# Twenty-four instead of twenty rounds of value sums beside the gates of a PEER layer

## The reference, cut to what matters

```python
experts = jnp.take_along_axis(cand_idx..., top_pos, axis=-1)   # 8 heads x 16 = 128 experts per token
gates = jax.nn.softmax(top_s, axis=-1)
def apply_block(args):                                         # one tile of 128 tokens
    xs, es, gs = args
    u = expert_u[es]; vv = expert_v[es]                        # tables of 16384 rows of 1024
    a = jax.nn.gelu(jnp.einsum('tkd,td->tk', u, xs), approximate=False)
    return jnp.einsum('tk,tkd->td', gs * a, vv)
```

## Time and profile before

| | us |
|---|---|
| median of 3 runs | 1929.65 (1924.39 to 1934.65) |
| the profiled execution | 1945.27 |
| its span | 1943.5 |
| around the span | 1.8 |
| PE busy | 1795.4 (92%) |
| DVE busy | 1292.2 (66%) |
| POOL busy | 896.7 (46%) |
| ACT busy | 293.5 (15%) |
| DMA moved | 670.21 MB, mean 345 GB/s |

### The profile page before, as it was taken

The page is one execution under the profiler, slowest core; times in us unless marked ns, Lnnn a source line. Parts: engine busy times, 40 slices in busy tenths (PEclk is TensorE's granted clock), DMA queues, the critical chain, the costliest instruction groups (busy, mean ns, idle before and its releaser), DMA issues.

```text
span 1943.5 us, 21544 instructions
## 1 busy us (share of the span) xinstructions
PE 1795.4 (92%) x8020; PEld 1152.3 (59%) x8020; DVE 1292.2 (66%) x2593; ACT 293.5 (15%) x661; POOL 896.7 (46%) x837
## 2 busy tenths in 40 slices
PE   4988898998999999998999999996889999999994
PEld 1666743554444359987888888884554444444441
DVE  2110476989579699998998975568875623336767
ACT  0120010555100001111111100005550000000000
POOL 1010225665456324334455555668865665435540
PEclk9999999999999999998999999998999999999998
DMA  8895859888999977559999999999989999999995
GB/s 360 338 370 214 344 160 394 291 286 324 392 324 363 390 272 298 187 192 362 366 361 375 386 387 409 405 394 329 327 308 409 409 409 409 409 409 409 409 410 203
DMA packets 168441, 670.21 MB, mean 345 GB/s; under 512 B 19563, under 2 KB 19691, under 8 KB 163085
## 3 DMA queue, kind: packets, MB, share of 16 engines
q0 software_dynamic: 112512, 410.79, 56.2%
q1 hardware_dynamic: 51072, 242.25, 31.8%
q10 hardware_dynamic: 4752, 15.81, 2.1%
HBM read 659.27 MB, written 7.39 MB: 343 GB/s over the span
## 4 chain that ended last, share of the span: by engine, by line
PE 46%; DMA 18%; DVE 18%; POOL 11%; issue 6%; ACT 1%; ACTq 0%; DVEq 0%; another core or an unknown queue 0%; POOLq 0%
PE psum L966 19%; POOL arena L566 11%; DMA arena<-in_expert_u_dram,arena 9%; DMA arena<-in_expert_v_dram,arena 4%; DVE arena L1511 4%; PE psum L751 4%; PE psum L992 3%; PE psum L995 3%; DVE psum L1784 3%; PE psum L740 2%; PE psum L1029 2%; DVE arena L1707 2%; DMA arena<-in_w_ada_dram 2%; PE psum L1006 2%; PE psum L1004 2%
## 5 line engine op out<-in xcount | busy, mean ns | idle before, releaser
L566 POOL DMA_INDIRECT arena<-in_expert_u_dram,arena x384 | 468.5, 1220 | 386.0 <-DVE arena L1511 261.6
L1511 DVE CUSTOM_DVE_ANT_0 arena<-arena 128x1024 f32<-128x1024 f32 x384 | 461.0, 1222 | 182.1 <-DMA arena<-in_expert_u_dram,arena 153.0
L566 POOL DMA_INDIRECT arena<-in_expert_v_dram,arena x384 | 390.7, 1018 | 357.9 <-DVE psum L1784 175.9
L1784 DVE SCALAR_TENSOR_TENSOR psum<-arena,psum 128x1024 f32<-128x1024 f32 x254 | 327.0, 1287 | 193.2 <-DMA arena<-in_expert_v_dram,arena 165.0
L893 PE MATMUL psum<-arena 128*128 128x256 f32 x2048 | 446.0, 381 | 7.3 <-DMA arena<-in_expert_uT_dram 7.3
L966 PE MATMUL psum<-arena 128*128 128x512 f32 x1024 | 443.7, 594 | 1.6 <-DMA arena<-in_expert_v_dram 1.6
L893 PEld LDWEIGHTS psum<-arena 128*128 128x128 f32 x2048 | 390.8, 191 | 61.3 <-issue 7.6
L966 PEld LDWEIGHTS psum<-arena 128*128 128x128 f32 x1024 | 193.3, 190 | 253.0 <-issue 249.0
L1064 PE MATMUL psum<-arena 128*128 128x128 f32 x1280 | 148.9, 278 | 2.1 <-DVE arena L1668 1.4
L1064 PEld LDWEIGHTS psum<-arena 128*128 128x128 f32 x1280 | 147.1, 194 | 3.6 <-issue 1.9
L1324 ACT ACTIVATE arena<-psum 128x512 f32<-128x512 f32 x64 | 38.2, 597 | 379.7 <-PE psum L893 292.6
(11 more groups left out here) (188 smaller groups left out, 1410.1 us busy)
## 6 DMA issues: line engine op xcount, KB each, us to landing
arena<-in_expert_uT_dram SPq DMA_DIRECT2D x128, 512.0 KB
arena<-in_expert_v_dram SPq DMA_DIRECT2D x128, 512.0 KB
arena<-in_w_ada_dram SPq DMA_DIRECT2D x12, 2048.0 KB
arena<-in_w_in_dram SPq DMA_DIRECT2D x11, 2048.0 KB
arena<-in_w_query_dram SPq DMA_DIRECT2D x8, 2048.0 KB, 22.7
arena<-in_w_in_dram SPq DMA_DIRECT2D x30, 512.0 KB, 7.9
arena<-in_w_o_dram SPq DMA_DIRECT2D x4, 2048.0 KB
arena<-in_expert_u_dram,arena POOLq DMA_INDIRECT x384
```

The source lines that it names most:

```text
L566: pool.indirect_dma_start(slot, None, table[0], bass.IndirectOffsetOnAxis(ap=number, axis=0)).then_inc(land, 16)
L1511: dve.tensor_tensor_reduce(UR[b], UR[b], U2B[e], 1.0, 0.0, ALU.mult, ALU.add, DOTS[e % 2][:, k:k + 1]).then_inc(u_free, 1)
L1784: dve.scalar_tensor_tensor(ys, row, weight, ys, ALU.mult, ALU.add).then_inc(v_free, 1)
```

## The change

`GATE_ROUNDS` becomes 24. So rounds 0 to 23 go beside the gates, three after each four batches, and rounds 24 to 31 go into the value stream. `ROUND_AFTER` before names the blocks 33, 35, 38, 42, 46, 50, 55, 59, 63, 67, 72 and 76; after it names 38, 40, 43, 47, 51, 55, 60 and 64. From the constants follow `BESIDE` (48 before, 32 after), `PACED_FROM` (76, then 64) and `PACE` (43, then 55), so the paced fetches are 96 in 55 blocks instead of 80 in 43. Both paces end at the same block, 119.

```diff
-SCORED_GROUPS, GATE_ROUNDS = 10, 20
+SCORED_GROUPS, GATE_ROUNDS = 10, 24
 BESIDE = ROUND * (ROUNDS - GATE_ROUNDS)
-ROUND_AFTER = {(33 + 2 * n if n < 2 else 38 + 17 * (n - 2) // 4): GATE_ROUNDS + n for n in range(ROUNDS - GATE_ROUNDS)}
+ROUND_AFTER = {(38 + 2 * n if n < 2 else 43 + 17 * (n - 2) // 4): GATE_ROUNDS + n for n in range(ROUNDS - GATE_ROUNDS)}
```

## The result

| | us | against before |
|---|---|---|
| before, 20 runs | 1929.35 (1921.31 to 1937.52) | |
| after, 20 runs | 1941.49 (1934.42 to 1947.20) | ratio 1.006, 95% interval 1.0048 to 1.0072 |
| forecast | 1935.6, range 1922 to 1949 | ratio 1.003 |

The change costs 12.1 us. By the interval of the ratio the cost is 9.3 to 13.9 us. That is in the range, but just over the 0.5% that the forecast called no change, to which it gave 52%: its likeliest case gave half of the loss.

What follows compares the result with a forecast made beforehand. It took POOL's unbroken issue to bound the gates, PE the value stream and late gathered values the tail; 21.5 - 7.4 + 1.5 - 9.6 = +6.0 us on the median 1929.65 gave 1935.6, range 1922 to 1949.

Steps and rivals of the forecast that it cites:

- What bounds the kernel now: POOL's unbroken issue, 6.37 us a round, sets the gates; PE paces the value stream; late gathered tile 2 values set the tail.
- Four more rounds beside the gates (+21.5): In the gates, POOL issues 16 more fetches and 4 weight copies that nothing hides: +21.5 us.
- the bounds: Price of four gate rounds: 20.5 us from undisturbed fetches, 25.5 us from the mean of the gates.
- Four fewer in the stream, and its start (-7.4 + 1.5): Value stream: PE saves 7.4 us on four rounds; score fetches ahead of first block loads cost 1.5 us.
- Rounds five blocks later (0): Value stream: starting late rounds five blocks later costs nothing, covered by the DMA's 20.5 us of slack.
- The tail (-9.6): After PE's end: a slower pace lands tile 2's last values earlier, so the tail is 10.5 us instead of 20.1.
- The first rival (the tail stays): End of the stream: last values still land late, the tail gives nearly nothing; +15.6 us, 1945; chance 22%.
- The second (the gates grow more): Gates: PE's clock falls after waits, slow rounds hold back buffers and POOL; +14 us, 1943.5; chance 13%.
- The third (the gates have cover): Gates: DVE's chain sets their length, so four rounds cost perhaps 5 us; -10.5 us, 1919; chance 10%.
- the fourth: Value stream: DMA, not PE, sets it, so it loses 20.5 us and the tail stays; +2.5, 1932; chance 7%.

Runs made afterwards that it cites:

- the second trace: The kernel before the change, traced again with no edit: its single execution took 1939.26 us.
- the PSUM runs: One-hot comparisons read their keys from PSUM instead of the SBUF copy; ratio to the kernel before 0.9957 with 20 gate rounds, 0.9945 with 24, 0.9912 with late rounds at 33 to 59.
- the first trace: The profiled execution of the changed kernel, with no further edit: 1935.52 us.
- the second, with shorter waits: The changed kernel traced again, no edit: 1943.26 us against 1931.29 for the kernel before, ratio 1.0066.
- the two longest gates traces: Changed kernel with late rounds at 33 to 59 and pace from 64 (160.2 us, ratio 1.0102), and with score fetches held until all gate rounds are summed (161.5 us, 1.007).

## Why the prediction came out as it did

**What bounds the kernel now: right.** Two readings were off without harm. The 2.0 us before the gate fetches were no wait for a used buffer: the row names no engine that ended them, and the second trace shows 0.3 us behind PE's sums. And the last value is summed 30.6 us after its fetch by the end of the sums; 29.3 us is to the start of the last one. POOL's issue beside the gates and the landing of tile 2's last values for the tail were each moved by an edit of their own and did what the trace had said. PE's own pace in the stream had no edit of its own; it is borne out by the stream getting 3.3 us shorter, and not 20.5, when 8.39 MB left it.

**Four more rounds beside the gates (+21.5): right on average**, +20.6, though single traces lie between 149.2 and 161.5 and the cost between 13.3 and 25.5 us by the pair compared. That the mean came so near is in part luck. The choice between the bounds was right as well, and for the reason given: the excess over 0.941 us of all fetches together is 23.7, 23.2 and 22.9 us for 80 fetches and 20.0, 23.3, 21.9, 25.0 and 21.6 for 96. Between 20 and 24 rounds it stays with DVE's 64 instructions and doesn't grow with the fetches. With 16 rounds it was only 13.3 us, but there the 16 weight copies took 13.4 us, 0.837 each instead of 0.3. Against the 0.21 us of a copy in the PSUM runs, fetches and copies together are delayed by some 23 us with 16 rounds, 26 with 20 and 22 to 31 with 24, an estimate that grows less than the number of fetches. The PSUM run shows which property of DVE's instructions matters: the second SBUF input. The Trainium skill (SBUF — State Buffer, "Who interferes with whom") has this rule of exclusion, and the traces agree. By the inference in the same section, that such an instruction leaves descriptor writing alone, the excess would have had another cause. But these indirect DMAs lost up to 1.07 us each, and lost it no more when one input came from PSUM. Whether the descriptor writing or another part of the fetch is held up isn't shown.

**Four fewer in the stream, and its start (-7.4 + 1.5): mis-sized.** -3.3 was measured instead of -5.9. The rounds' own 7.4 us did go, but PE waited 3.4 to 4.6 us for its first blocks. I had costed the four score fetches that run ahead. I had not seen that the first block's load starts only after the last `place`, and that before the change its landing was covered by PE's wait for the last round (2.45 us) and by that round at half speed (3.52 us instead of 1.92). Nor had I counted the clock: in the first trace it was granted at 0.70 in the first ten microseconds behind the wait of 4.62 us, some 3 us more. In the second, with shorter waits, it stayed at 1.00, and the stream was 3.9 us shorter.

**Rounds five blocks later (0): right for PE, wrong for the kernel.** No late round waited for its fetches. But I named the DMA's 20.5 us of slack as the cover and counted the same slack a second time in the tail. I had even written that POOL and DMA go idle there, and priced it at nothing. Most of the slack was spent ahead of block 38, where POOL issued nothing for 32 us and the DMA fell to 203 GB/s, and the five blocks were missing from the pace. Giving them back gained 8.4 us, of the 12 that the change costs. In the sum their price stands in the tail, which could have been 7.4 us.

**The tail (-9.6): the mechanism right, the size off.** -5.8 was measured. The steps: value 32 waited 7.3 us from fetch to sum (6.5 forecast); the seven loads for the finishes raised that to 15 within the next four fetches (15.5 forecast); over the rest of the pace it grew by 8 us, to 22.8, where 1.44 MB against 1.41 gave 4. The difference of two nearly equal rates was the weakest number of the sum.

The first rival (the tail stays) had named this place and was half right. The second (the gates grow more) shows in size in the two longest gates traces, 160.2 and 161.5 us, but not by its mechanism: POOL's waits behind PE's sums stayed at 1.8 and 1.9 us there. The third (the gates have cover) falls by POOL's row, and the fourth by the stream, which lost 3.3 us and not 20.5. The error of 6 us in the sum is 3.8 from the tail and 2.6 from the stream, both of which I had put on the good side of their bounds; the gates and the spread of the executions make up the rest. The measured +12.1 lies nearer to the prices of the first two rivals (+15.6 and +14) than to the +6.0 of the forecast. So it was the width of the range, more than the sum, that held it.

## What to carry to other kernels

When work is moved out of a stage with two full resources, ask of each separately where its slack appears. Bytes freed ahead of a wait do nothing for a queue that builds up behind it, so give the freed time to the part that is paced. Cover found as busy shares (DVE 118 of 128 us beside POOL's 105) says little: look for the engine that issues without a pause, and count instructions per unit of work on each. Count a resource's slack as cover only once. Where GpSimd issues gathers beside DVE instructions with two SBUF inputs, try one input from PSUM first.

## What the runs showed of the hardware

A GpSimd indirect DMA of 128 rows of 4 KB issues in 0.94 us; beside DVE comparisons with two SBUF inputs (1.22 us each, two in every 3.6 us) a third of them (29 of 80) took 1.1 to 2.01 us. With one input in PSUM they took 0.955 on average, and gathers alone then moved 402 GB/s with 24 rounds, where the changed kernel moved 351 and the kernel before 331: what had looked like the rate of gathers was the rate of their issue. That was unexpected, since a DMA share of 0.93 beside 331 GB/s looks like a nearly full DMA.

Left open: why the gates of the same code took 149 to 161 us. In the two longest (161.5 and 160.2), POOL shows 4.2 and 4.4 us of waits that the profile can't name. Its fetches took 5.0 and 1.6 us longer in all than in the shortest, and its weight copies 3.9 and 4.3 us. That is most of the difference, and what caused it isn't shown. Open too is why the tail with 20 rounds fell from 20 to 16.7 us with the keys in PSUM.
